# Sums of squares ahead of five input projections: eight operands added on VectorE, one unit sum on TensorE in the fifth tile

## The reference

```python
def rms_norm(x, w):
    xf = x.astype(jnp.float32)
    y = xf * lax.rsqrt(jnp.mean(xf * xf, -1, keepdims=True) + RMS_EPS)
    return (y * w.astype(jnp.float32)).astype(x.dtype)
...
for i in range(DEPTH):                      # first stack
    a_in = rms_norm(hs, norm_w[i, 0])
    mix = gated_deltanet(a_in, ...) if i % 2 == 0 else mlstm(a_in, ...)
    hs = hs + keep * rms_norm(mix, norm_w[i, 1])
    f = conv_ffn(rms_norm(hs, norm_w[i, 2]), ...)
    hs = hs + keep * rms_norm(f, norm_w[i, 3])
...
for layer in range(DEPTH):                  # second stack
    y = mixer(x @ w_in) @ w_out
    x = layer_norm(ALPHA * x + y, ...)
    x = layer_norm(ALPHA * x + swiglu(x, w_gate, w_up, w_down), ...)
```

## Time and profile before

| | |
|---|---|
| time, median of 3 runs | 1445.23 us (1445.07 to 1447.6) |
| span of the profiled execution | 1443.1 us (of its own time no more than this is shown) |
| TensorE busy | 1423.5 us, 99% of the span, 11333 matmul records |
| TensorE weight loads | 1363.9 us |
| VectorE busy | 1013.4 us, 70% |
| ScalarE busy | 779.4 us, 54% |
| GpSimd busy | 294.0 us, 20% |
| DMA | 223.57 MB, mean 155 GB/s |

### The profile page before, as it was taken

The page is one execution under the profiler, slowest core; times in us unless marked ns, Lnnn a source line. Parts: engine busy times, 40 slices in busy tenths (PEclk is TensorE's granted clock), DMA queues, the critical chain, the costliest instruction groups (busy, mean ns, idle before and its releaser), DMA issues.

```text
span 1443.1 us, 31771 instructions
## 1 busy us (share of the span) xinstructions
PE 1423.5 (99%) x11333; PEld 1363.9 (95%) x11333; DVE 1013.4 (70%) x1701; ACT 779.4 (54%) x1399; POOL 294.0 (20%) x348
## 2 busy tenths in 40 slices
PE   9999999999999999999999999999999999999997
PEld 8999888899999999999999999999999989999986
DVE  7884957659876477569888477587664687776645
ACT  6556324556655366466565356464453567654542
POOL 3804002103444000002544000013330012033310
PEclk9999999999999999999999999999999999999999
DMA  7551231244655535344666544546556433565552
GB/s 256 177 175 47 88 101 47 93 142 160 190 175 175 175 119 189 103 146 128 193 189 189 182 134 152 164 146 200 183 168 204 152 116 118 163 217 186 183 180 91
DMA packets 60996, 223.57 MB, mean 155 GB/s; under 512 B 6768, under 2 KB 6896, under 8 KB 60528
## 3 DMA queue, kind: packets, MB, share of 16 engines
q1 hardware_dynamic: 60624, 220.17, 48.1%
q10 hardware_dynamic: 288, 2.23, 0.4%
HBM read 221.32 MB, written 1.05 MB: 154 GB/s over the span
## 4 chain that ended last, share of the span: by engine, by line
PE 81%; DVE 12%; issue 3%; ACT 3%; DVEq 1%; ACTq 0%; POOL 0%; POOLq 0%
PE bank L440 20%; PE bank L441 20%; PE bank L442 20%; DVE wlo L415 3%; PE bank L461 2%; PE bank L1168 2%; PE bank L462 1%; PE bank L468 1%; DVE bank L947 1%; PE bank L3284 1%; PE bank L3285 1%; PE bank L3287 1%; ACT cv L831 1%; DVE cv L839 1%; DVE work L1782 1%
## 5 line engine op out<-in xcount | busy, mean ns | idle before, releaser
L415 DVE TENSOR_TENSOR wlo<-raw,whi 128x1024 fp32r<-128x1024 f32 x397 | 501.4, 1268 | 249.3 <-ACT whi L410 248.8
L410 ACT ACTIVATE whi<-raw 128x1024 fp32r<-128x1024 f32 x397 | 415.1, 1056 | 288.6 <-PE bank L442 240.6
L440 PE MATMUL bank<-xs,whi 128*128 128x258 f32 (+2 forms) x1984 | 569.2, 287 | 0.0
L441 PE MATMUL bank<-xs,whi 128*128 128x258 f32 (+2 forms) x1984 | 563.9, 284 | 0.0
L442 PE MATMUL bank<-xs,wlo 128*128 128x258 f32 (+2 forms) x1984 | 561.6, 283 | 0.0
L440 PEld LDWEIGHTS bank<-xs,whi 128*128 128x128 f32 x1984 | 374.2, 189 | 3.0 <-issue 1.6
L442 PEld LDWEIGHTS bank<-xs,wlo 128*128 128x128 f32 x1984 | 375.0, 189 | 0.0
L441 PEld LDWEIGHTS bank<-xs,whi 128*128 128x128 f32 x1984 | 374.3, 189 | 0.6 <-issue 0.2
L440 PE MATMUL bank<-hf,whi 128*128 (+3 forms) x848 | 241.3, 285 | 2.0 <-DVE cv L839 0.8
L441 PE MATMUL bank<-hf,whi 128*128 (+3 forms) x848 | 240.3, 283 | 0.0
L442 PE MATMUL bank<-hf,wlo 128*128 (+3 forms) x848 | 240.2, 283 | 0.0
(11 more groups left out here) (516 smaller groups left out, 1671.8 us busy)
## 6 DMA issues: line engine op xcount, KB each, us to landing
raw<-stream SPq DMA_DIRECT2D x412, 512.0 KB, 3.7
con<-consts SPq DMA_DIRECT2D x1, 1284.5 KB, 10.5
big<-mla ACTq DMA_DIRECT2D x1, 1152.0 KB, 7.8
hs_sb<-hs SPq DMA_DIRECT2D x2, 544.0 KB, 4.2
work<-last ACTq DMA_DIRECT2D x1, 1024.0 KB, 9.1
y_out<-work SPq DMA_DIRECT2D x4, 256.0 KB, 2.0
par<-params SPq DMA_DIRECT2D x1, 420.0 KB, 7.9
par<-params SPq DMA_DIRECT2D x1, 224.0 KB, 4.8
```

The costliest lines, as they stand in the source:

```text
L410: nc.scalar.activation(whi[:, s, :], raw[:, s, :], ACT.Copy).then_inc(hi_split, 1)
L415: nc.vector.tensor_tensor(wlo[:, s, :], raw[:, s, :], whi[:, s, :].bitcast(F32), ALU.subtract).then_inc(block_split, 1)
L440: nc.tensor.matmul(out_, whi[:, slot, w], hi, start=start, stop=False)
L441: nc.tensor.matmul(out_, whi[:, slot, w], lo, start=False, stop=False)
```

## The change

VectorE adds the two sums of four as well (`eight_sum`), behind the low half of tile 4 and ahead of the low half of tile 5. TensorE then needs one unit sum where it had two, and it stands in tile 4 (the fifth) ahead of group k = 2, where the two stood in tile 3 ahead of k = 6. Tile 4 is taken out of the loop for that, which begins with tile 5: in the up phases four turns and seven tiles written out, where it was five turns; in `ml_in` one turn and nothing behind it, where it was one turn and one tile. This is done in up0, ml_in, up1, up2 and up3. The two other places with sums of four (`gdn_in` and `od_in`) stay as they were.

```diff
             for k in range(KC):
-                if between and k == 6:
+                if between and k == 2:
                     between(pe)
...
         if behind:
-            tile(AHEAD, 0, behind)
-            head = AHEAD + 1
+            tile(AHEAD)
+            tile(AHEAD + 1, 0, behind)
+            head = AHEAD + 2
...
+    def eight_sum(dve, name, T, lo=0):
+
+        v = S("norm", "dve")
+        dve.wait_ge(*v.at(f"{name}_four{KC - 1}"))
+        nc.vector.tensor_tensor(sq[:, KC - 1, lo:T], sq[:, 3, lo:T], sq[:, KC - 1, lo:T], ALU.add).then_inc(*v.mark(f"{name}_eight"))
+
...
-    def fours_behind(name, g, T, lo=0):
-
-        def src(m):
-            return "dve", f"{name}_four{m}", sq[:, m, lo:T]
-
-        return lambda pe: sums_pe(pe, name, src, g, ((3, True, False), (7, False, True)), T, lo)
+    def eight_behind(name, g, T, lo=0):
+
+        src = lambda m: ("dve", f"{name}_eight", sq[:, m, lo:T])
+
+        return lambda pe: sums_pe(pe, name, src, g, ((KC - 1, True, True),), T, lo)
...
         split_lo(dve, fifth(phase))
+        eight_sum(dve, name, T1, t.start)
         split_lo(dve, sixth(phase))
...
         if phase and phase != "od_in":
+            eight_sum(dve, name + "v", T2)
             split_lo(dve, sixth(phase))
```

More of the change, by code:

```diff
@@ L3478, in _ @@
         gdn_pe(pe)
-        ln_behind = lambda n: fours_behind(f"ln{n}v", G[f"lv{n}"], T2)
-        behind = lambda name: fours_behind(name, G[name], T1, PRE_FIRST[name])
+        ln_behind = lambda n: eight_behind(f"ln{n}v", G[f"lv{n}"], T2)
+        behind = lambda name: eight_behind(name, G[name], T1, PRE_FIRST[name])
         ln_wave = lambda n: fours_in_wave(pe, f"ln{n}v", G[f"lv{n}"], T2)
```

## The result

The changed kernel takes 1450.0 us (median of 6 runs, 1449.48 to 1451.85) where the kernel before takes 1445.03 (6 runs, 1444.79 to 1447.6): ratio 1.0029, 95% interval 1.0019 to 1.0039. It is slower by 5.0 us; forecast were 3.9 us and a time of 1449.1. The span of the profiled execution is 1448.0 us, 4.9 more than before. Executions of either kernel, and of the others here, fall for the most part into two groups some 2.6 us apart (in four of the profiled ones TensorE's granted clock is 0.50, the lower of its two levels, for 3 to 7 us from about 119 us on, ahead of the first of the five places), so medians of few runs move by that; the places are therefore compared within a trace, each from the first matmul of its wave (L461).

A forecast was written before the change was run, and what follows sets the result against it. TensorE was taken to bound the kernel, with late low halves next. Five places' losses, saved sums included, made 3.86 us; 1445.2 + 3.9 = 1449.1 us, 0.27% slower, range 1446.2 to 1451.2.

The forecast's parts named there:

- What bounds the kernel: Whole kernel: TensorE busy 99% of the span; the narrower place is how near low halves of next weights come to tile starts.
- What is removed: Five places: one unit sum fewer in each, together 2.2 us of TensorE, 0.15% of the time.
- The add costs nothing: VectorE, five places: adds of 0.36 us each, covered by 0.5 us in up0; without cover 1.8 us in all.
- Tile 4 meets its low half: Tile 4 waits in up0, ml_in, up1; TensorE keeps only about 0.2, 0.1, 0.15, 0.43, 0.43 us of the saved sum.
- The scale comes later, and the delay is passed on in full: Scale from the moved sum: 1.29 us later in up0, 1.34 ml_in, 1.28 up1, 1.00 up2 and up3, all reaching VectorE's scaled tiles.
- Where TensorE then stops: Tile 7 (up0, up1) or 6 (ml_in, up2, up3) waits: losses 1.18, 1.10, 1.28, 0.15, 0.15 us, sum 3.86.
- Behind that nothing is lost: Later in each phase VectorE waits for TensorE again, so the phase ends later by TensorE's loss and no more.
- The loop's new limits cost nothing: TensorE's loop: no cost that a row shows; its one L440 wait put down to issue is 0.4 us in the run.
- The hidden scale: Rival: unseen slack of 1.0 to 1.3 us per place between scale and low half hides the delay; 1443.9 us, chance 0.28.
- the last rival: TensorE also stops for written-out tiles (1.6 us) or the add in tile 4 (1.0 us); up to 1451.7 us, chance 0.14.

## Why the prediction was right

*What bounds the kernel* held: TensorE, with the low halves of tiles 6 and 7 next to it.

*What is removed*: 2.2 us of unit sums was right; putting the second sum back delays tile 5 by 0.42 to 0.46 us at each place.

*The add costs nothing* held in the changed kernel, by the cover that was named: the sum stands late enough, and VectorE waits for the scale behind it. The run with the add ahead of tile 4's low half shows the price without that cover: 0.48 us of delay on VectorE, not 0.36, since the add waits for the end of the sum ahead of it, and 0.16 to 0.25 us of waiting on TensorE in up0, ml_in and up1.

*Tile 4 meets its low half* held: from the wave it starts 0.76 us earlier in up0 where 0.77 was forecast, 0.64 (0.65) in ml_in and 0.67 (0.68) in up1, and 0.87 in up2 and up3, with no wait there.

*The scale comes later, and the delay is passed on in full*: low halves of tiles 6 and 7 come 1.30, 1.34, 1.30, 1.00 and 1.00 us later (1.29, 1.34, 1.28, 1.00, 1.00). The run with the scale alone delayed and the run with the sum at k = 6 show that this is the cause.

*Where TensorE then stops* held at each place, to 0.1 us. In up0 and up1 tile 6 waits as well, ahead of the tile that sets the loss. The rows are tile 6 of ml_in, tile 7 of up1, and tile 6 of up2, where TensorE catches up with the low half, so that the sum it saved is spent in waiting:

```profile
546.58 0.39 PE L440 MATMUL bank<-xs,whi 128*128 128x272 f32 x1 [0.85 <-DVE wlo L415]
...
679.08 0.38 PE L440 MATMUL bank<-xs,whi 128*128 128x258 f32 x1 [0.60 <-DVE wlo L415]
...
965.33 0.38 PE L440 MATMUL bank<-xs,whi 128*128 128x258 f32 x1 [0.33 <-DVE wlo L415]
```

*Behind that nothing is lost* was right for the phases: VectorE waits for TensorE 11 times in up0 as before. It was 1.0 us short for the whole kernel, by the terms above that lie outside the five places; the sum had none of them. So the agreement in the five places, 3.82 us against 3.86, bears out the mechanism, and the forecast of the time is as near as it is only because these terms are small. "The loop's new limits cost nothing" is true at the limits (the run with tile 4 out of the loop); the pause in od_in came with the longer program, and such a cost I had put among the rivals, at other places.

*The rivals.* The hidden scale fell: not a tenth of a microsecond of slack was found between scale and low half. It missed because a less busy engine's result decided when the busiest one could go on. Of the last rival, the wait for the add did not come, and a pause put down to issue came, in od_in.

## What to carry to other kernels

A saving on the engine that bounds the kernel counts only if nothing that it waits for moves back: here 2.2 us of TensorE's work went, and a scale that came 1.0 to 1.3 us later cost 3.8 us net. Before moving an instruction later on a full engine, follow who waits for its result, round to the engine itself, and compare the delay with the slack at the tile that closes the circle: it is read off the trace as end of the low half against start of the tile. The add was free where it stood ahead of a wait of VectorE that was longer than the add, and where TensorE reached the sum after it; where either failed, in up0, ml_in and up1 of the run with the sum in tile 3, it took back the gain.

## What the runs showed of the hardware that was not expected

TensorE paused 0.69, 0.78 and 1.17 us in three executions at the same matmul of straight code with nothing in the profile to wait for; with 384 more instructions ahead of it the pause was gone. Idle time of TensorE can be followed by a lower clock: behind the wait of 1.86 us in up1 (sum at k = 6) and the pause of 1.17 us in od_in the granted clock was 0.50 for 3.4 us, some 15 matmuls with 0.21 to 0.22 us from start to start instead of 0.12, about 1.4 us by estimate. Behind the pauses of 0.69, 0.78 and 0.99 us, and behind waits of 1.8 and 2.3 us in up0 and ml_in, it stayed at 1.00; what decides was not settled. VectorE shows a shorter pause: in all traces with the add in up0, ml_in and up1, its fourth add behind down1 starts 0.89 us behind the third where it is 0.53 us in the other traces, and the idle time is named after a ScalarE instruction that had ended earlier; TensorE starts the next wave some 0.3 to 0.4 us later. The row is from the changed kernel:

```profile
849.08 0.42 DVE L721 TENSOR_TENSOR sq<-sq 128x256 f32<-128x256 f32 x1 [0.46 <-ACT sq L702]
```

It is not there in the traces without that add. What it waits for was not settled.
